# The start address of the weight slots modulo 256 bytes: 64 in place of 128

## What is computed

```python
def first_block(x, ...):               # 16 meta rows in front: 272 rows
    proj = rmsnorm(h, norm1_g) @ w_in                  # 1024 -> 4096
    u, q, k, v, g_ssm, g_att = split(proj)
    y_ssm = s5_mixer(u, ...)                           # state space, glu_w
    y_att = rmsnorm(diff_attention(q, k, v), subln_g)
    mixed = sigmoid(g_ssm) * (y_ssm @ w_ssm_out) + sigmoid(g_att) * (y_att @ w_att_out)
    h = h + mixed @ w_o
    return h + conv_glu_ffn(rmsnorm(h, norm2_g), w_up, conv_w, conv_b, w_down)
...
def second_block(x, ...):
    z = rms_norm(x, norm_mix) @ w_in                   # RG-LRU, HGRN2, MoBA groups
    x = x + concat(ya, yb, yc) @ w_out
    u = square(relu(rms_norm(x, norm_mlp) @ w_ff1))    # 1024 -> 4096
    return rms_norm(x + u @ w_ff2, norm_final)
```

## Time and profile before

| | us |
|---|---|
| median of 3 runs | 733.09 (732.58 to 735.19) |
| the execution that was profiled | 735.88 |
| its span, first to last instruction | 734.1 |
| TensorE busy with matmuls | 706.6 (96%) |
| TensorE busy with weight loads | 663.5 (90%) |
| VectorE, ScalarE, GpSimd busy | 537.2, 386.8, 24.3 |

### The profile page before, as it was taken

The page is one execution under the profiler, slowest core; times in us unless marked ns, Lnnn a source line. Parts: engine busy times, 40 slices in busy tenths (PEclk is TensorE's granted clock), DMA queues, the critical chain, the costliest instruction groups (busy, mean ns, idle before and its releaser), DMA issues.

```text
span 734.1 us, 14582 instructions
## 1 busy us (share of the span) xinstructions
PE 706.6 (96%) x6152; PEld 663.5 (90%) x6152; DVE 537.2 (73%) x954; ACT 386.8 (53%) x587; POOL 24.3 (3%) x50
## 2 busy tenths in 40 slices
PE   6999999999999999999999999999889999999996
PEld 4988998888999999999999889888779998998995
DVE  5899798556978877776777889965767665666653
ACT  6487368366365454444446664587654434434431
POOL 3010000000000000000000320000000000000000
PEclk9999999999999999999999999999999999999999
DMA  8751153133555555555655553333346565565541
GB/s 241 207 171 59 59 172 117 60 112 119 172 173 173 185 200 190 173 177 196 199 175 173 179 172 116 116 115 116 115 125 194 190 210 172 184 215 175 179 165 57
DMA packets 94700, 115.66 MB, mean 158 GB/s; under 512 B 7971, under 2 KB 83932, under 8 KB 94636
## 3 DMA queue, kind: packets, MB, share of 16 engines
q1 hardware_dynamic: 94244, 114.51, 48.2%
q0 software_dynamic: 128, 0.13, 0.1%
q10 hardware_dynamic: 264, 0.10, 0.1%
HBM read 113.69 MB, written 1.05 MB: 156 GB/s over the span
## 4 chain that ended last, share of the span: by engine, by line
PE 78%; DVE 10%; ACT 7%; issue 3%; DMA 1%; SPq 0%; DVEq 0%; ACTq 0%
PE psum L1805 17%; PE psum L1806 16%; PE psum L1807 16%; PE psum L2344 4%; PE psum L2342 4%; PE psum L2343 4%; DVE w_lo L1081 4%; ACT w_hi L500 3%; PE psum L2111 2%; PE psum L2113 2%; PE psum L2109 2%; PE psum L1917 1%; PE psum L1952 1%; DMA xtok<-in_x_dram 1%; PE psum L2167 1%
## 5 line engine op out<-in xcount | busy, mean ns | idle before, releaser
L1081 DVE TENSOR_TENSOR w_lo<-w_raw,w_hi 128x2048 fp32r<-128x2048 f32 x105 | 239.4, 2288 | 72.0 <-ACT w_hi L500 71.8
L500 ACT ACTIVATE w_hi<-w_raw 128x2048 fp32r<-128x2048 f32 x105 | 199.0, 1906 | 54.4 <-PE psum L2344 36.6
L1805 PE MATMUL psum<-x2n_hi,w_hi 128*128 128x256 f32 x400 | 114.5, 286 | 2.6 <-DVE x2n_lo L1532 1.3
L1806 PE MATMUL psum<-x2n_lo,w_hi 128*128 128x256 f32 x400 | 112.0, 280 | 0.0
L1807 PE MATMUL psum<-x2n_hi,w_lo 128*128 128x256 f32 x400 | 111.9, 280 | 0.0
L1805 PE MATMUL psum<-hs_hi,w_hi 128*128 128x256 f32 (+1 forms) x352 | 99.5, 283 | 0.0
L1806 PE MATMUL psum<-hs_lo,w_hi 128*128 128x256 f32 (+1 forms) x352 | 99.1, 281 | 0.0
L1807 PE MATMUL psum<-hs_hi,w_lo 128*128 128x256 f32 (+1 forms) x352 | 98.9, 281 | 0.0
L1805 PEld LDWEIGHTS psum<-x2n_hi,w_hi 128*128 128x128 f32 x400 | 75.3, 188 | 5.9 <-DVE x2n_lo L1532 2.3
L1807 PEld LDWEIGHTS psum<-x2n_hi,w_lo 128*128 128x128 f32 x400 | 76.1, 190 | 0.0
L1806 PEld LDWEIGHTS psum<-x2n_lo,w_hi 128*128 128x128 f32 x400 | 75.2, 188 | 0.6
(11 more groups left out here) (439 smaller groups left out, 1520.8 us busy)
## 6 DMA issues: line engine op xcount, KB each, us to landing
w_raw<-in_w_ff_dram SPq DMA_DIRECT2D x32, 1024.0 KB, 5.3
w_raw<-in_w_in_dram SPq DMA_DIRECT2D x27, 1024.0 KB, 5.3
w_raw<-in_w_up_dram SPq DMA_DIRECT2D x22, 1024.0 KB, 5.1
w_raw<-in_w_down_dram SPq DMA_DIRECT2D x11, 1024.0 KB, 4.9
w_raw<-in_w_o_dram SPq DMA_DIRECT2D x4, 1024.0 KB, 5.4
w_raw<-in_w_out_dram SPq DMA_DIRECT2D x4, 1024.0 KB, 5.2
w_raw<-in_w_ssm_out_dram SPq DMA_DIRECT2D x2, 1024.0 KB, 5.1
w_raw<-in_w_att_out_dram SPq DMA_DIRECT2D x2, 1024.0 KB, 5.0
```

The source lines that it names most:

```text
L500: A.activation(w_hi[:, u % NW, :], raw[:, u % NRAW, :], ACT.Copy).then_inc(sem("hi_ready"), 1)
L1081: V.tensor_tensor(w_lo[:, u % NRAW, :], raw[:, u % NRAW, :], w_hi[:, u % NW, :].bitcast(F32), ALU.subtract).then_inc(sem("lo_ready"), 1)
L1805: T.matmul(out_, lh, rh, start=start, stop=False)
L1806: T.matmul(out_, lh, rl, start=False, stop=False)
```

## The change

`base` grows by 192 and the gap of 192 bytes that stood between `p_b` and `C1` goes away. Everything from `C1` on, and so R and all activations, keeps its address. The tiles in front of it move up by 192 bytes: `w_raw`/`w_lo`, `w_hi`, `CT`, `ident`, `ones`, `sel`, `selT`, `p_a` from 128 to 64 modulo 256, and `p_b` from 0 to 192. No instruction is added, removed or moved on any engine; only operand addresses differ.

```diff
-        base = 16512
+        base = 16512 + 192
         top = [base]
...
         p_b = sb("p_b", [P, 2, 2, KEYS_B])
-        top[0] += 192
         C1 = sb("C1", [P, NP1])
```

## The result

| | before | changed |
|---|---|---|
| median, lowest and highest | 733.02 us (732.58 to 735.19) | 742.59 us (741.46 to 742.88) |
| ratio to before, 95% interval | | 1.0118 [1.0096, 1.0140] |
| the execution that was profiled | 735.88 us, span 734.1 | 742.88 us, span 741.1 |

The changed kernel is slower by 9.6 us of the medians. The forecast was 737.8, that is 4.7 more, so the direction was right and the size about half of what came. 742.59 lies just inside the range of 726 to 743, but above the forecast's own range of 736 to 742, in the stretch that had a chance of 0.05. Of the two profiled executions the changed one is longer by 7.0 us, since the profiled execution of before was one of its longer ones.

What follows compares the result with a forecast made beforehand. TensorE, stepping between matmuls nearly without waits, was taken to bound the kernel. Terms of 4.2 + 1.2 - 0.7 = 4.7 us on 733.09 gave 737.8 us, with a range of 726 to 743 and the forecast's own 736 to 742.

Steps and rivals of the forecast that it cites:

- What bounds the kernel: Whole kernel: TensorE, busy 96% of the span with matmuls, steps from one to the next nearly without waits.
- D: Moving operand's start minus stationary operand's, modulo 256; place said to be worth up to 8 ns in three 272-column matmuls.
- First term: 2,448 matmuls of 256 columns, weights stationary, distance -64 to 0: 1.7 ns more each, 4.2 us lost.
- Second term: up_a and w_o, 720 matmuls taken at 258 columns, about the same move: 1.7 ns more each, 1.2 us lost.
- Third term: ff2, 384 matmuls of 512 columns, weights moving, distance 0 to -64: 1.7 ns less each, 0.7 us gained.
- Fourth part: u, k, q, gate and v units: the same four distances come in another order, so 0.
- Fifth: glu, ssm_out, att_out and tok units of w_in_2, 384 matmuls: 0.7 us of unknown sign, taken as 0.
- Sixth and seventh: VectorE and ScalarE splits with small tiles, then DMAs into the weight slots: each 0; DMAs could gain up to 2.9 us.
- equal places favour the fast pace: Rival, 2,448 matmuls of 256 columns: slow steps become fast, 4.5 ns each, 724.3 or 728.7 us; chance 0.25 for 724 to 731.
- places do not matter: Rival, all matmuls: the start's place has no effect by itself, 733.1 us; chance 0.25 for 731 to 735.5.
- The fourth case: Rival, 256-column matmuls: the 20% at fast pace lose 2.2 us more, 740.0 us; within the 0.45 for 736 to 742.
- a whole step of 4.5 ns more: 256-column matmuls: the pace steps up as a whole, 11.0 us lost, 744 to 745 us; chance 0.05 for 742 to 746.

Runs made afterwards that it cites:

- all_down64: Every tile, weight slots and activations alike, 64 bytes lower than in the kernel before, all operand distances kept: 732.77 us, ratio 0.998.
- act_down192: All activations 192 bytes lower than in the kernel before, weight slots in place, giving the changed kernel's operand distances: 742.52 us, ratio 1.012.

## Why the prediction was right in direction and half in size

- **What bounds the kernel**: right. TensorE steps without a wait nearly everywhere, and the change works on these steps. VectorE's and ScalarE's splits (2,228 to 2,293 and 1,894 to 1,920 ns after, before) did not move.
- **D, not the own place, is the lever**: right, by the rotated pattern and by `all_down64` and `act_down192`. The rows for it were read with one of the four places left out: at 35.46 us, with `xn` at 0 (D = -128), the three durations are 292 + 290 + 290 = 872 ns, so the place was worth 10 ns and not 8, and at 272 columns D = 0 is not the worst.
- **First term, 2,448 matmuls at 256 columns: +4.2 forecast, +7.4 measured.** The mechanism was right and the term mis-sized. The 1.7 ns from 272 columns was near the distance to the slow pace (117.9 to 120.0 is 2.1 ns, 5.1 us). What failed is that I left the fast pace in place and put its loss (2.2 us) into a rival: at D = 0 it is all but gone. The two belonged together, in one term of 4.2 + 2.2.
- **Second term, 720 matmuls at 258 columns: +1.2 forecast, -0.4 measured.** The step that failed was to carry the 1.7 ns from 272 columns over to 258. The order of the distances is another for each column count, as the table shows.
- **Third term, ff2: -0.7 forecast, +2.6 measured.** The largest error, and of sign. The hint was there that ff2 stepped at twice the fast pace and so might have nothing left to gain; I took the gain that symmetry gives nonetheless. The bound of 1.7 us was too low as well: D = -64 costs 6.8 ns a step there, more than the 4.5 between the paces of 256 columns.
- **Fourth part (u, k, q, gate, v): 0 forecast, -0.1 measured.** Right, the four values were only dealt out anew. **Fifth**: within the 0.7 us named. **Sixth and seventh**: right at 0. By the Trainium skill (DMA: Bandwidth & Descriptors, How a descriptor splits into AXI transactions), whose rule is one for what a descriptor reads, loads would by an estimate from its beats have become a twentieth shorter if it held for the slots that they write as well. The median from issue to landing of the w_ff loads is 5.3 us before and after, so the trace does not show it.
- **A term that the sum did not have: the waits.** Longer steps shorten the waits behind them. In the profiled executions the steps took 9.6 us and the span 7.0. Against the 4.7 us of the forecast for that execution (740.6, measured 742.88) the error is thus smaller than on the medians, where the lower runs of the kernel before come on top; why those are lower is open.
- **The rivals.** That equal places favour the fast pace was wrong: it vanished. That places do not matter, with the rule of the Trainium skill on separate read ports (TensorE: Matmul & The Clock Gate, Part 2), fell with `act_down192`: at 256 columns the step is 120.0 ns at D = 0 and 113.4 to 117.9 at D = -64, with nothing but the distance between the streamed and the loaded operand changed, so the two do get in each other's way for these 4-byte operands. The fourth case, the fast pace lost as well, priced at 740.0, came nearest in kind.
- **The range** held by 0.4 us, and that is luck. Its upper end came from the case of a whole step of 4.5 ns more in the 256-column units, which did not come (3.0 ns in the mean); ff2, for which the sum had a gain, brought the time up there instead.

## What to carry to other kernels

Where each fp32r matmul has its own weight load and 256 columns or more, look at the distance modulo 256 bytes between moving and stationary operand: it was worth up to 6% of a step at 256 columns and 3% at 512, nothing at 192 and 224, and here 1.2% of the kernel, with no instruction changed. Moving one buffer moves the distance for every matmul that reads it, so group the matmuls by column count and by which side the buffer is on, and size each group by a row with the same column count; values do not carry over from 272 columns to 258 or 512. Where a stage already runs at the best pace seen anywhere, as ff2 did, take a loss for more likely than a gain. And read a stage's step again after a change beside it, since a neighbour's pace is carried over (226.7, 227.8 or 229.5 ns in ff2 at one and the same distance).

## What the runs showed that I had not expected

- The same matmuls at the same addresses run at 113.3 or at 117.6 ns a step, in two profiles of the same kernel, and keep the pace as long as the row of them is not broken.
- With 512 columns moving the best distance is 0 (226.7 ns) and nearly all others cost 6.5 ns (233.1 to 233.5), the reverse of 256 columns.
- Cutting the moving columns from 256 to 192 shortens a step by 2 ns from its fast pace: below 256 columns something else than the stream, most likely the weight load of 128 x 128 fp32r numbers, sets it at about 111 ns.
- ff2, with its columns and addresses unchanged, steps at 229.5 instead of 226.7 ns when the units beside it stream 192 columns.
